# Query-key dots in float32r with split operands instead of float32 on half the array

## The chip, the cores and the metric

One core of a Trainium2 chip runs the whole program in one launch. The metric is the device time of that launch in microseconds, the median of several runs. A separate profiled execution gives the trace from which all rows below are taken.

## The reference, cut to what matters

Two layers run over a prompt of 1024 tokens and a sample of 64 tokens with 256 cached ones. In each layer the input projection feeds, among others, a ReLU indexer (4 heads of 64, one shared key), whose scores pick the top 256 keys, and a sparse attention (8 query heads of 64 over 2 key heads):

```python
rel = jax.nn.relu(jnp.einsum('bqhd,bsd->bqhs', qi_b, ki).astype(jnp.float32))
score = jnp.einsum('bqhs,bqh->bqs', rel, wi_b.astype(jnp.float32)) * IDX_SCALE
_, idx = lax.top_k(score, topk)
...
logits = jnp.einsum('bqngd,bqknd->bqngk', qg, kg).astype(jnp.float32) * (HD_A ** -0.5)
```

The retention heads, the gates, the norms and the output projection are not touched.

## The kernel before, in words

The work is a fixed sequence of 180 steps, 9 tiles of 128 tokens (t = 0 to 7 the prompt, t = 8 the sample) for each of 10 column groups in 2 layers: idx (324 columns), ret four times, gate, att twice, out twice. The order on every engine is written out by hand: a loop over i, in which TensorE projects the tile of step i+1 in four quarters (q = 0 to 3, two slices of the contraction each) and puts the work of older steps between the quarters. `project` makes each product in three float32r matmuls (high by high, low by high, high by low; the sample tile needs two).

A tile of idx or att goes this way. TensorE projects it; VectorE rotates it (`rope`, lines 1720 to 1737, through the scratch tile by_cos_sin); TensorE turns queries and keys in quarter 2 (line 996, into out_bank for idx, a turn bank for att); ScalarE copies them out (`take_turn`, lines 1363 and 1364) into queries and keys; in quarters 0 to 3 of the next i TensorE makes the dots (`dot_keys`, line 1044), always two heads at a time. One head's 64 features lie in partitions 0 to 63, the other's in 64 to 127, and a dot is one float32 matmul over its half. A tile has one or two parts of at most 512 keys; with one part there are dots in quarters 0 and 2, with two parts in all four. I call the dots of one part and two heads a pair. There are 22 pairs in the idx group of a layer and 26 in each att group, 148 in all: 72 of 512 keys, 32 of 384, 20 of 256, 4 of 320 and 20 of 128.

idx dots are taken by ScalarE (ReLU, line 1403) and weighed by VectorE (line 1756). att dots are masked and maximised by VectorE (line 1928). GpSimd makes the low halves of the weights (line 1554) and, in the idx groups, the low halves of the normed input h (line 1560, two for a tile), and the diagonals by which the raw input is normed while it is turned (lines 1593 to 1601). The weights of the next column group come one slice a step, t = 0 to 7, into w_hi and w_lo with 16 places (WS).

## Time and profile before

| what | us |
|---|---|
| median of 3 runs | 1431.36 (1430.39 to 1431.76) |
| the profiled execution | 1430.55 |
| its span, first to last instruction | 1428.7 |
| TensorE busy in it | 1380.3 (97%) |
| VectorE busy | 1010.9 (71%) |
| ScalarE busy | 783.7 (55%) |
| GpSimd busy | 405.2 (28%) |

Busy times of TensorE are modelled: matmuls overlap in the pipeline, so that the distance from one start to the next says more of the cost than the duration of one. A float32 matmul is two instructions in the trace. In a row of the timeline the first number is the start in us from the start of the span, the second the duration.

### The profile page before, as it was taken

The page shows a single profiled execution, that of the slowest core. Times are in us where ns is not written, and L with a number is a line of the kernel's source. Part 1 is how long each engine was busy: PE and PEld are TensorE (multiplying, and loading weights), DVE is VectorE, ACT ScalarE, POOL GpSimd, SP SyncE. Part 2 cuts the span into 40 slices and gives each one's busy share as a digit, 9 for nine tenths or more (in the row PEclk, how much of TensorE's full clock was granted, in tenths as well). Part 3 has the DMA queues.
Part 4 walks back from the last instruction along what each step waited for, and adds up shares of the span by engine and source line. Part 5 has one row for each costly group of instructions (what it writes and reads, how often), then busy time and mean ns, then how long its engine had stood idle before and what let it go on. Part 6 is the DMA issues. An engine that isn't in the chain of part 4 may idle for free.

```text
span 1428.7 us, 24483 instructions
## 1 busy us (share of the span) xinstructions
PE 1380.3 (97%) x7623; PEld 1054.7 (74%) x7623; DVE 1010.9 (71%) x2991; ACT 783.7 (55%) x1916; POOL 405.2 (28%) x382
## 2 busy tenths in 40 slices
PE   6999999999999999999988999999999999999997
PEld 2865777788887677668877587877888766766786
DVE  0787899999996555542398789999999754554225
ACT  2555666666326665664454566666632566666432
POOL 3741332444421011001387123443343100100110
PEclk9999999999999999999999999999999999999999
DMA  9743333211232112223252111211223211221325
GB/s 317 230 133 106 96 121 115 78 29 54 58 92 66 42 39 69 82 65 106 93 186 62 40 32 51 52 43 40 62 58 88 68 32 46 71 66 61 116 78 175
DMA packets 125191, 122.05 MB, mean 85 GB/s; under 512 B 33256, under 2 KB 94024, under 8 KB 125064
## 3 DMA queue, kind: packets, MB, share of 16 engines
q1 hardware_dynamic: 124608, 120.36, 28.1%
q8 instruction: 64, 1.05, 0.3%
q14 instruction: 63, 0.52, 0.1%
q10 hardware_dynamic: 456, 0.13, 0.0%
HBM read 93.55 MB, written 26.90 MB: 84 GB/s over the span
## 4 chain that ended last, share of the span: by engine, by line
PE 55%; DVE 33%; issue 5%; POOL 2%; DMA 2%; ACT 1%; DVEq 0%; ACTq 0%; SPq 0%; POOLq 0%
DVE U L1782 12%; PE proj L1017 10%; PE proj L1018 9%; PE turn L996 9%; PE proj L1020 9%; PE logit L1044 7%; PE out_bank L1071 5%; PE spare L1044 2%; DVE turned L1737 2%; DVE by_cos_sin L1722 2%; DVE by_cos_sin L1720 2%; DVE probsT_more L1855 2%; DVE probsT_more L1859 1%; POOL h_lo L1560 1%; DVE U L1876 1%
## 5 line engine op out<-in xcount | busy, mean ns | idle before, releaser
L1017 PE MATMUL proj<-w_hi,h_hi 128*128 128x512 f32 (+2 forms) x1440 | 574.4, 399 | 3.0 <-POOL h_lo L1560 2.2
L1018 PE MATMUL proj<-w_lo,h_hi 128*128 128x512 f32 (+2 forms) x1440 | 535.3, 372 | 0.0
L1020 PE MATMUL proj<-w_hi,h_lo 128*128 128x512 f32 (+2 forms) x1280 | 477.4, 373 | 0.0
L1554 POOL TENSOR_TENSOR w_lo<-w_raw,w_hi 128x512 fp32r<-128x512 f32 (+2 forms) x160 | 202.9, 1269 | 741.5 <-ACT w_hi L1260 741.3
L1017 PEld LDWEIGHTS proj<-w_hi,h_hi 128*128 128x128 f32 x1440 | 271.9, 189 | 53.3 <-issue 15.8
L1018 PEld LDWEIGHTS proj<-w_lo,h_hi 128*128 128x128 f32 x1440 | 272.1, 189 | 31.0
L1020 PEld LDWEIGHTS proj<-w_hi,h_lo 128*128 128x128 f32 x1280 | 240.2, 188 | 37.1
L1782 DVE TENSOR_SCALAR_CACHE_REDUCE U<-score,cand 128x384 bf16<-128x384 f32 x310 | 223.0, 752 | 2.4 <-DVE cand L1799 0.3
L1044 PE MATMUL logit<-keys,queries 64*128 64x512 f32 (+4 forms) x454 | 137.2, 542 | 2.3 <-ACT U L1403 1.6
L1383 ACT ACTIVATE probsT_more<-turn 128x512 f32<-128x512 f32 (+3 forms) x156 | 76.1, 491 | 96.0 <-PE turn L996 95.8
L996 PEld LDWEIGHTS turn<-ident,U 128*128 128x128 f32 x604 | 68.4, 140 | 52.7 <-issue 36.9
L996 PE MATMUL turn<-ident,U 128*128 128x128 f32 x604 | 97.4, 281 | 4.2 <-ACT probsT_more L1383 2.6
L1260 ACT ACTIVATE w_hi<-w_raw 128x512 fp32r<-128x512 f32 (+2 forms) x160 | 95.0, 595 | 11.4 <-DMA w_raw<-in_w_in_dram 11.4
L1416 ACT ACTIVATE U<-U,neg_max 128x384 f32<-128x384 f32 (+7 forms) x108 | 81.5, 755 | 23.5 <-DVE neg_max L1933 23.1
L1570 POOL TENSOR_TENSOR rstd<-means,minus_half 128x3 f32<-128x3 f32 (+2 forms) x42 | 32.2, 766 | 215.6 <-DVE means L1910 148.9
L1435 ACT ACTIVATE U<-score,cand 128x896 bf16<-128x896 f32 x62 | 64.6, 1043 | 34.6 <-DVE cand L1820 34.6
L1737 DVE TENSOR_TENSOR turned<-by_cos_sin 128x256 f32<-128x256 f32 (+1 forms) x126 | 71.6, 568 | 9.6
L1720 DVE TENSOR_TENSOR by_cos_sin<-rows,cos_b 128x256 f32<-128x256 f32 (+1 forms) x108 | 52.2, 484 | 35.9 <-ACT rows L1316 33.1
L1928 DVE CUSTOM_DVE_ANT_0 U<-logit,score 128x512 f32<-128x512 f32 (+3 forms) x71 | 41.2, 585 | 49.1 <-PE logit L1044 48.9
L1071 PE MATMUL out_bank<-probsT_more,U 128*64 128x256 f32 x468 | 75.2, 385 | 0.0
L1435 ACT ACTIVATE probsT_more<-score,cand 128x1024 bf16<-128x1024 f32 x62 | 70.4, 1136 | 0.0
L1044 PEld LDWEIGHTS logit<-keys,queries 64*128 64x128 f32 x454 | 44.4, 184 | 30.9 <-issue 27.8
(203 smaller groups left out, 2109.0 us busy)
## 6 DMA issues: line engine op xcount, KB each, us to landing
w_raw<-in_w_in_dram SPq DMA_DIRECT2D x80, 256.0 KB, 3.3
probsT_more<-in_w_ada_dram SPq DMA_DIRECT2D x64, 256.0 KB, 3.9
score<-mixed_dram SPq DMA_DIRECT2D x36, 256.0 KB, 3.0
score<-in_w_ada_dram SPq DMA_DIRECT2D x32, 256.0 KB, 5.1
w_raw<-in_w_out_dram SPq DMA_DIRECT2D x32, 256.0 KB, 3.4
U<-in_x_prompt_dram SPq DMA_DIRECT2D x12, 512.0 KB, 4.1
mixed_dram<-U SPq DMA_DIRECT2D x24, 192.0 KB, 2.1
gates_dram<-U SPq DMA_DIRECT2D x18, 256.0 KB, 2.1
```

The source lines that it names most:

```text
L996: ins = nc.tensor.transpose(ring.bank(key)[:, n * P:(n + 1) * P], piece, ident[:])
L1017: nc.tensor.matmul(out, h_hi[:, k, tile], hi, start=(k == 0), stop=False)
L1018: ins = nc.tensor.matmul(out, h_hi[:, k, tile], lo, start=False, stop=(t == SAMPLE and k == KT - 1))
L1020: ins = nc.tensor.matmul(out, h_lo[:, k, tile], hi, start=False, stop=(k == KT - 1))
L1044: ring.filled(nc.tensor.matmul(ring.bank(key)[:, 0:m], queries[rows_, HILO[g] % 2, h // 2, :], keys[rows_, k0 + a:k0 + a + m], start=True, ...
L1071: ins = nc.tensor.matmul(out_bank[HD * pair:HD * pair + HD, 0:256], v, probsT[part + pair][:, :, b * P:(b + 1) * P], start=(kb == 0), stop ...
L1260: nc.scalar.activation(w_hi[:, s % WS, 0:w], w_raw[:, n % RAWS, 0:w], ACT.Copy).then_inc(w_hi_ready, 1)
L1416: nc.scalar.activation(probs[n % 4][:, 0:w], probs[n % 4][:, 0:w], ACT.Exp, bias=neg_max[:, n % 4:n % 4 + 1], scale=ATT_SCALE, accum_out=r ...
L1435: nc.scalar.activation(tested[n % 2][:, 0:valid_keys(t)], scores(t)[:, 0:valid_keys(t)], ACT.Sign, bias=cand[:, col:col + 1].bitcast(F32) ...
L1554: nc.gpsimd.tensor_tensor(w_lo[:, s % WS, 0:w], w_raw[:, n % RAWS, 0:w], w_hi[:, s % WS, 0:w].bitcast(F32), ALU.subtract).then_inc(w_lo_re ...
L1737: signal(nc.vector.tensor_tensor(turned[:, ro % 2, 0:w], by_cos[:, 0:w], by_sin[:, 0:w], ALU.add), rope_done, ro + 1)
L1782: ins = nc.vector.tensor_scalar(found[:, n % 2, 0:valid_keys(t)], s, cand[:, j:j + 1].bitcast(F32) if b else 0.0, extra(t), ALU.is_ge, ALU ...
```

## The change

Keys are kept as a high and a low half in float32r (keys_hi, keys_lo), and a head's queries as one 128-row operand: its high half in the partitions it came in, its low half in the other 64. The turned keys already stand twice, in both halves of the partitions. A dot is then two float32r matmuls over all 128 rows, by keys_hi and by keys_lo, with the same queries. ScalarE first copies the turned tile raw into by_cos_sin (line 1419 of the changed kernel), then makes the high halves of the queries in two copies. GpSimd makes both halves of the keys (1630, 1632). The low halves of the queries are made by GpSimd in idx steps (1643, two subtractions) and by VectorE in att steps (1854, two). `rope` of the next tile uses the same scratch, so it waits for all of these. The two key halves need room, so WS goes from 16 to 14 and the last two slices of a column group (LATE = 2) are split only in the sample step of the group before, after its first quarter.

```diff
-WS = 2 * KT
+WS = 2 * KT - 2
+LATE = 2 * KT - WS
...
-        keys = sb("keys", [P, NKEYS])
-        queries = sb("queries", [P, 2, GROUP // 2, P])
+        keys_hi = sb("keys_hi", [P, NKEYS], F32R)
+        keys_lo = sb("keys_lo", [P, NKEYS], F32R)
+        queries = sb("queries", [P, 2, GROUP, P], F32R)
...
+        raw_turn = by_cos_sin[:, 0:384]
...
-                    rows_ = slice(HD * (h % 2), HD * (h % 2) + HD)
-                    ring.filled(nc.tensor.matmul(ring.bank(key)[:, 0:m], queries[rows_, HILO[g] % 2, h // 2, :],
-                                                   keys[rows_, k0 + a:k0 + a + m], start=True, stop=True), key)
+                    out, both_halves = ring.bank(key)[:, 0:m], queries[:, HILO[g] % 2, h, :]
+                    nc.tensor.matmul(out, both_halves, keys_hi[:, k0 + a:k0 + a + m], start=True, stop=False)
+                    ring.filled(nc.tensor.matmul(out, both_halves, keys_lo[:, k0 + a:k0 + a + m],
+                                                 start=False, stop=True), key)
...
-                    turns_of(g).wait_taken(pe, ("q", g))
+                    wait_queries_split(pe, HILO[g] + 1)
+                    pe.wait_ge(keys_split, HILO[g] + 1)
...
-                nc.scalar.activation(queries[:, HILO[g] % 2], src[:, 0:256].rearrange("p (h n) -> p h n", n=P), ACT.Copy)
-                ring.take(nc.scalar.activation(keys[:, blk * P:(blk + 1) * P], src[:, 256:384], ACT.Copy), ("q", g))
+                ring.take(nc.scalar.activation(raw_turn, src[:, 0:384], ACT.Copy), ("q", g))
+                ring.wait_taken(act, ("q", g))
+                for half in (0, 1):
+                    at = slice(HD * half, HD * half + HD)
+                    ins = nc.scalar.activation(queries[at, n % 2, half::2, :],
+                                               raw_turn[at, 0:256].rearrange("p (h n) -> p h n", n=P), ACT.Copy)
+                ins.then_inc(queries_high, 1)
...
-                if i + 1 < STEPS:
-                    if weight_slice(i + 1) is not None:
-                        split_weights(weight_slice(i + 1))
+                if early_slice(i + 1) is not None:
+                    split_weights(early_slice(i + 1))
                 for q in range(QUARTERS):
+                    if q == 1:
+                        for s in late_slices(i + 1):
+                            split_weights(s)
...
+                if kind(i) in ("idx", "att"):
+                    split_keys(i)
+                if kind(i) == "idx":
+                    lower_queries(i)
+                if has_cache_turn(i):
+                    split_cache(i)
...
+                if splits_before(g):
+                    wait_queries_split(dve, splits_before(g))
+                    dve.wait_ge(keys_split, splits_before(g))
...
+                if kind(i) == "att":
+                    lower_queries(i)
```

TensorE, the dots of quarter 0 of an idx tile with 512 keys, between two quarters of the projection of a later tile (logit is one of two banks). Before, then after:

```order
L1020 MATMUL proj<-w_hi,h_lo 128x324
L1044 MATMUL logit<-keys,queries 128x512 [waits logit_taken1,logit_taken0,idx_turn_taken]
L1044 MATMUL logit<-keys,queries 128x512
L1017 MATMUL proj<-w_hi,h_hi 128x324 [waits w_lo_ready]
L1018 MATMUL proj<-w_lo,h_hi 128x324
```

```order
L1066 MATMUL proj<-w_hi,h_lo 128x324
L1092 MATMUL logit<-keys_hi,queries 128x512 [waits logit_taken0,logit_taken1,keys_split,index_split]
L1093 MATMUL logit<-keys_lo,queries 128x512
L1092 MATMUL logit<-keys_hi,queries 128x512
L1093 MATMUL logit<-keys_lo,queries 128x512
L1063 MATMUL proj<-w_hi,h_hi 128x324 [waits w_lo_ready]
```

Two matmuls became four, and the wait on ScalarE's copy became one on GpSimd's keys and low queries.

GpSimd, one step of the idx group of the first layer (the three operations on input_mean, input_root and score make one diagonal). Before, then after:

```order
L1601 TENSOR_SCALAR score<-ident,input_root 128x128 [waits input_rooted,turn_full0]
L1554 TENSOR_TENSOR w_lo<-w_raw,w_hi 128x512 [waits w_hi_ready]
L1560 TENSOR_TENSOR h_lo<-U,h_hi 128x4x128 [waits h_hi_ready] x2
L1593 TENSOR_SCALAR input_mean<-squares 128x1 [waits x_squared]
L1596 TENSOR_TENSOR input_root<-input_mean,minus_half 128x1 [waits input_summed]
```

```order
L1614 TENSOR_TENSOR w_lo<-w_raw,w_hi 128x512 [waits w_hi_ready]
L1620 TENSOR_TENSOR h_lo<-U,h_hi 128x4x128 [waits h_hi_ready] x2
L1630 CAST keys_hi<-by_cos_sin 128x128 [waits idx_turn_taken]
L1632 TENSOR_TENSOR keys_lo<-by_cos_sin,keys_hi 128x128 [waits keys_high]
L1643 TENSOR_TENSOR queries<-by_cos_sin,queries 64x2x128 [waits keys_split,queries_high]
L1643 TENSOR_TENSOR queries<-by_cos_sin,queries 64x2x128 [waits index_split]
L1690 TENSOR_SCALAR input_mean<-squares 128x1 [waits x_squared,index_split]
```

Four operations stand behind the two low halves of h and ahead of everything of the next step.

VectorE, the first tile of the first att group. The operations on probsT_more and ties are the last selection mask. Before, then after:

```order
L1720 TENSOR_TENSOR by_cos_sin<-rows,cos_b 128x320 [waits rope_done,proj_taken]
L1722 TENSOR_TENSOR by_cos_sin<-rows,sin_b 128x320
L1735 TENSOR_TENSOR turned<-by_cos_sin 128x64 [waits dve_done,key_stored1,turn_full0]
L1737 TENSOR_TENSOR turned<-by_cos_sin 128x320
L1851 TENSOR_SCALAR probsT_more,ties<-score,cand 128x320 [waits rope_done]
```

```order
L1845 TENSOR_TENSOR turned<-by_cos_sin 128x320
L1854 TENSOR_TENSOR queries<-by_cos_sin,queries 64x2x128 [waits queries_high]
L1854 TENSOR_TENSOR queries<-by_cos_sin,queries 64x2x128
L1972 TENSOR_SCALAR probsT_more,ties<-score,cand 128x320 [waits queries_split]
L1973 TENSOR_SCALAR probsT_more<-score,cand 128x320
```

The two subtractions wait for the turn of this very tile, and the last mask now stands behind them.

## Rows read from the trace of the kernel before

**Rows 1.** Windows by stage: stretch, length, each engine's busy us, TensorE's granted clock.

```profile
38.74:127.90 89.16, 85.20 (x529) 61.21 (x529) 71.64 (x155) 47.46 (x124) 43.84 (x47) 1.00 0.53 160
419.44:651.96 232.52, 230.00 (x1454) 165.68 (x1452) 130.54 (x427) 146.12 (x381) 23.09 (x19) 1.00 0.21 59
743.04:829.10 86.06, 78.18 (x435) 55.70 (x434) 68.73 (x140) 44.27 (x111) 37.09 (x34) 1.00 0.23 58
```

**Rows 2.** Timeline of TensorE in an att step; start, us, line, tiles, shapes, count.

```profile
501.86 0.34 PE L1020 MATMUL proj<-w_hi,h_lo 128*128 128x384 f32 x1
502.04 0.60 PE L996 MATMUL turn<-ident,U 128*128 128x128 f32 x4
502.57 0.69 PE L1044 MATMUL logit<-keys,queries 64*128 64x512 f32 x1
502.57 0.69 PE L1044 MATMUL spare<-keys,queries 64*128 64x512 f32 x1
503.10 0.59 PE L1044 MATMUL logit<-keys,queries 64*128 64x512 f32 x1
...
503.63 0.55 PE L996 MATMUL turn<-ident,U 128*128 128x128 f32 x3
...
505.59 1.13 PE L1044 MATMUL logit<-keys,queries 64*128 64x512 f32 x4
...
511.48 0.34 PE L1020 MATMUL proj<-w_hi,h_lo 128*128 128x384 f32 x1
511.75 0.69 PE L1044 MATMUL logit<-keys,queries 64*128 64x512 f32 x1
```

**Rows 3.** Timeline of TensorE, two float32r matmuls of 512 columns.

```profile
643.24 0.39 PE L1020 MATMUL proj<-w_hi,h_lo 128*128 128x512 f32 x1
643.47 0.40 PE L1017 MATMUL proj<-w_hi,h_hi 128*128 128x512 f32 x1
```

**Rows 4.** Groups by shape, GpSimd and VectorE: count, busy us, mean ns, idle before.

```profile
L1554 POOL TENSOR_TENSOR w_lo<-w_raw,w_hi 128x512 fp32r<-128x512 f32 x112 | 147.7, 1319 | 579.8 <-ACT w_hi L1260 579.7
L1554 POOL TENSOR_TENSOR w_lo<-w_raw,w_hi 128x324 fp32r<-128x324 f32 x16 | 14.3, 902 | 15.9 <-ACT w_hi L1260 15.9
L1601 POOL TENSOR_SCALAR score<-ident,input_root 128x128 f32<-128x128 f32 x9 | 5.6, 622 | 1.4 <-POOL input_root L1596 1.2
```

```profile
L1953 DVE TENSOR_TENSOR score<-score 128x256 f32<-128x256 f32 x36 | 15.3, 426 | 3.7
```

**Rows 5.** Timeline of an idx step of the first layer (tile 4).

```profile
83.77 0.39 ACT L1363 ACTIVATE queries<-out_bank 128x256 f32<-128x256 f32 x1
...
84.18 1.17 ACT L1268 ACTIVATE h_hi<-U 128x512 fp32r<-128x512 f32 x2
...
84.92 2.52 POOL L1560 TENSOR_TENSOR h_lo<-U,h_hi 128x512 fp32r<-128x512 f32 x2 [3.68 <-ACT h_hi L1268]
...
87.54 0.70 PE L1044 MATMUL logit<-keys,queries 64*128 64x512 f32 x2
```

**Rows 6.** Chain of work, idx group of the second layer: start, us, what.

```profile
754.20 2.90 POOL h_lo L1560 x2
...
760.14 2.47 POOL h_lo L1560 x2
...
768.32 1.60 DVE turned L1737
```

**Rows 7.** Timeline of an idx step of the second layer (tile 3).

```profile
779.23 0.39 ACT L1363 ACTIVATE queries<-out_bank 128x256 f32<-128x256 f32 x1
...
780.64 0.70 PE L1044 MATMUL logit<-keys,queries 64*128 64x512 f32 x2
```

**Rows 8.** Timeline, first tile of the first att group.

```profile
428.12 0.38 ACT L1363 ACTIVATE queries<-turn 128x256 f32<-128x256 f32 x1 [3.34 <-PE turn L996]
...
430.10 0.49 PE L1044 MATMUL logit<-keys,queries 64*128 64x128 f32 x4
...
430.33 1.30 DVE L1720 TENSOR_TENSOR by_cos_sin<-rows,cos_b 128x320 f32<-128x320 f32 x1
```

More of the change, by code:

```diff
@@ L304, in weight_slice, with early_slice, late_slices @@
     return (C + 1) * KT + t if t < KT and C + 1 < DEPTH * NCH else None
+def early_slice(g):
+    return weight_slice(g) if 0 <= g < STEPS and g % NT < KT - LATE else None
+def late_slices(g):
+    return [weight_slice(g - n) for n in range(LATE, 0, -1)] \
+        if 0 <= g < STEPS and g % NT == SAMPLE and g // NT + 1 < DEPTH * NCH else []
 def raw_items():
@@ L627, in build @@
         turn_taken = [sem(f"turn_taken{n}") for n in range(RB)]
+        queries_high = sem("queries_high")
+        queries_split = sem("queries_split")
+        index_split = sem("index_split")
+        keys_high = sem("keys_high")
+        keys_split = sem("keys_split")
+        cache_high = sem("cache_high")
+        cache_split = sem("cache_split")
+        first_quarter = sem("first_quarter")
         idx_turned = sem("idx_turned")
@@ L678, in ring_of, with cache_ordinal, splits_before, wait_queries_split @@
             return att_logits if kind(g) == "att" else logits
+        def cache_ordinal(g):
+            return sum(1 for k in range(g + 1) if has_cache_turn(k))
+        def splits_before(g):
+            return sum(1 for k in HILO if k < g)
+        def wait_queries_split(eng, n):
+            last = [g for g in HILO_STEPS[:n]]
+            index = 2 * sum(1 for g in last if kind(g) == "idx")
+            if index:
+                eng.wait_ge(index_split, index)
+            if len(last) * 2 > index:
+                eng.wait_ge(queries_split, len(last) - index // 2)
         def hidden_half(l, t, u):
@@ L761, in wait_keys_free, with wait_cache_free @@
                         ring_of(j).wait_full(eng, ("l", j, 3, len(key_parts(held)) - 1))
+        def wait_cache_free(eng, g):
+            if HILO[g] >= NT:
+                j = HILO_STEPS[HILO[g] - NT + 1]
+                n = valid_keys(SAMPLE) if kind(j) == "idx" else blocks_of(SAMPLE)[1] * P
+                ring_of(j).wait_full(eng, ("l", j, 3, len(key_parts(n)) - 1))
         def raw_value(n):
@@ L877, in _ @@
                     l, c, t = lct(i + 1)
-                    before = [k for k in range(i + 1) if has_cache_turn(k)]
-                    if before:
-                        turns.wait_full(sp, ("cache", before[-1]))
+                    if cache_ordinal(i):
+                        sp.wait_ge(cache_split, cache_ordinal(i))
                     src = cache_kidx_a[l, 0] if kind(i + 1) == "idx" else cache_k_a[l, 0, :, c - ATT0, :]
@@ L1020, in project @@
                         ins = nc.tensor.matmul(out, h_lo[:, k, tile], hi, start=False, stop=(k == KT - 1))
+                if quarter == 0 and t == SAMPLE:
+                    ins.then_inc(first_quarter, 1)
                 if quarter == QUARTERS - 1:
@@ L1257, in split_weights @@
                 act.wait_ge(raw_landed[n % RAWS], raw_value(n))
-                if C >= 2:
+                if s % KT >= KT - LATE and C:
+                    act.wait_ge(first_quarter, C)
+                elif C >= 2:
                     act.wait_ge(proj_done, (C - 1) * NT)
@@ L1281, in take_projection @@
                     act.wait_ge(rope_done, sum(1 for k in ROPE if k < g))
+                    if splits_before(g):
+                        wait_queries_split(act, splits_before(g))
+                        act.wait_ge(keys_split, splits_before(g))
                     nc.scalar.activation(sample_low[:, 0:w], src[DEC:P, 0:w], ACT.Copy).then_inc(low_copied, 1)
@@ L1643, in _ @@
                     lower_hidden(0, 1)
-                if i + 1 < STEPS and weight_slice(i + 1) is not None:
-                    lower_weights(weight_slice(i + 1))
+                if early_slice(i + 1) is not None:
+                    lower_weights(early_slice(i + 1))
+                for s in late_slices(i + 1):
+                    lower_weights(s)
                 for l, t in hidden_turns(i - 1):
@@ L1738, in rope, with lower_queries @@
                        rope_done, ro + 1)
+            def lower_queries(g):
+                n = HILO[g]
+                dve.wait_ge(queries_high, n + 1)
+                for half in (0, 1):
+                    have, other = (slice(HD * h, HD * h + HD) for h in (half, 1 - half))
+                    ins = nc.vector.tensor_tensor(queries[other, n % 2, half::2, :],
+                                                  raw_turn[have, 0:256].rearrange("p (h n) -> p h n", n=P),
+                                                  queries[have, n % 2, half::2, :].bitcast(F32), ALU.subtract)
+                    if half == 0:
+                        do(ins)
+                signal(ins, queries_split, ATT[g] + 1)
             def weigh_relus(g, q):
```

49 lines of the change are left out of this document (40 added, 9 removed).

## The prediction

> **What bounds the kernel now.** I read the windows by stage first, then TensorE's timeline. The windows say that TensorE is the bound almost everywhere: in the first layer's attention (two att groups and their tail) it is busy 230.0 of 232.5 us, while VectorE, ScalarE and GpSimd have 130.5, 146.1 and 23.1 [rows 1]. The second layer's attention is the same. In the idx group of layer 0 TensorE has 85.2 of 89.2 us; in that of layer 1 only 78.2 of 86.1, and the chain there runs over GpSimd's low halves of h, from 754 on, and then over VectorE's rotation at 768 [rows 6]. So a microsecond less on TensorE is a microsecond less of time in the att groups, and not in the opening of the idx groups.
>
> The timeline gives what a pair of dots costs. Both heads start at the same 502.57, their second instructions at 503.10, and the next turn starts at 503.63: a pair of 512 keys holds TensorE 1.06 us [rows 2]. The four records of such a pair take 1.13 from first start to last end [rows 2], those of a pair of 128 keys 0.49 [rows 8], so 384 keys cost 0.64, and a pair of 384, 256 and 128 costs 0.85, 0.63 and 0.42. Getting in costs extra: a projection matmul of 384 columns passes in 0.18 (501.86 to 502.04), but the last before dots takes 0.27 (511.48 to 511.75); and of four turns that take 0.11 each the last takes about 0.20 (502.04 to 502.57 is 0.53) [rows 2]. That is 0.09 a pair. On the way out three turns end a full 0.55 after their start, against 0.60 for four [rows 2], some 0.06 more than in a stream. I read this as the price of going between the full array and its two halves.
>
> **What TensorE gains.** Four float32r matmuls replace the pair. One of 512 columns passes in 0.23 [rows 3], one of 384 in 0.18, so by the 0.055 for 128 columns one of 256 in 0.12; one of 128 columns I put at 0.11, the pace of the turns, since its weights have to come in too. Pairs of 512, 384, 256 and 128 then cost 0.92, 0.70, 0.48 and 0.44: gains of 0.14, 0.15, 0.15 and -0.02. The operands have all 128 rows like the projection's, so I take it that the 0.09 in and the 0.06 out go too: 0.29, 0.30, 0.30 and 0.13 a pair. The 104 att pairs (48 of 512, 24 of 384, 16 of 256, 16 of 128) give 13.9 + 7.2 + 4.8 + 2.1 = **28 us**, the 44 idx pairs (24, 8, 4, 4, and 4 of 320) 7.0 + 2.4 + 1.2 + 0.5 + 1.2 = **12 us**. The trace shows no float32r matmul under 324 columns; were the short ones four times as dear as by width, 20 pairs would cost 0.4 more, 8 us. If the way in and out stays as dear as now, the att gain is 13 us.
>
> The Trainium skill speaks against this edit. "TensorE: Matmul & The Clock Gate", Part 3, says that small matmuls on different row groups run concurrently, at some 4 ns between starts, and "FP8 and Floating Point Precision", TensorE Precision Notes, counts four passes for float32. By these two the pair costs 4 x 512 / 2.4 GHz = 0.85 us (an estimate) and four float32r matmuls as much, so nothing is gained. The trace agrees on the concurrency (502.57 twice) and not on the sum, 1.06.
>
> **The link that is added, att.** Counted from ScalarE's copy (line 1363), the dots were ready 0.65 later. Now the raw copy of 384 takes some 0.50 (256 take 0.38 in rows 8, 128 more add 0.11), a wait on it 0.1, two copies of 64 partitions 0.7: 1.3. Then VectorE's two subtractions, 0.43 each by a 256-wide one [rows 4], give 2.2; beside them GpSimd makes the keys in 1.2. TensorE comes to the dots 1.98 after the copy in tile 0 of the first att group [rows 8]; later tiles have more work between, so I cost them at nothing, the cover being a quarter of projection and the values. In tile 0, VectorE also waits for the turn of this tile, with the last mask queued behind it: its rotation is over before the turn, and the high halves come 1.3 after 428.12, so it stands idle some 2 us and works 0.9 more, and the next rotation, at 430.33 before, comes that much later [rows 8]. I put 3 us a layer on this, **6 us**, between 1 and 10.
>
> **The same link, idx.** Here GpSimd does four operations in a row. 512 columns take it 1.32, 324 take 0.90 [rows 4], so 256 take about 0.8 and 128 about 0.55; the cast, between nothing known and the 0.62 of a 128-wide scaling [rows 4], 0.5. With the two of 256 that is 2.65, and with three hand-overs of 0.1 some 3.1 us (bounds 2.4 and 4.0, as VectorE gets in between).
>
> Layer 0: the four stand behind two low halves of h, which wait for ScalarE, which makes them after the queries. In tile 4, the copy starts at 83.77 and GpSimd's halves at 84.92 for 2.52 [rows 5]. ScalarE's part is 0.65 longer now, so those end at 88.1 and the four at 91.2; TensorE stood at the dots at 87.54 [rows 5], now 0.3 earlier. It waits 4.0 us. Five tiles (2 to 6) have this shape: 19 us. Tiles 7 and 8 have no halves of h ahead, 1 us. Tiles 0 and 1 have no dots, but the next rotation waits for the four: 3.5 us each. Together 27, less 6 gained: **+21 us**.
>
> Layer 1: the chain is on GpSimd already [rows 6], and the four operations of tiles 0, 1 and partly 2 are inserted in it: 3.1 + 3.1 + 1.8 = 8. From tile 3 on the dots came 1.41 after the copy [rows 7], and they need 0.5 + 0.1 + 3.1 = 3.7 now, less 0.3 that TensorE comes sooner: 2.5 us of wait, shrinking to about 1 at tile 8, 11 us for six tiles. Together 19, less 6: **+13 us**. VectorE's rotation, held by GpSimd in this stretch (1.60 for 320 columns where 256 take 0.43 elsewhere [rows 4, 6]), is likely to be held more often; I leave that in the bounds.
>
> The Trainium skill has the mechanism: "SBUF — State Buffer" calls the port pair of VectorE and GpSimd an exclusive lock, which a VectorE instruction with two SBUF inputs takes too. By that each of GpSimd's four could also wait for one of VectorE's; the 4.0 above covers it.
>
> **Late slices.** ScalarE gets two weight copies and GpSimd two subtractions (2 x 1.32, rows 4) in one step instead of two. They are needed a full step later, so the weights are not late; ScalarE's queue is. 19 times 0.15 us: **+3 us**, between 0 and 8.
>
> **Sum.** -28 + 6 + 21 + 13 + 3 = +15 on the profiled 1430.55, which is 1445.6. The median was 0.8 above the profiled run, so 1446.
>
> **Rivals.** (a) The link is hidden better than I think: GpSimd's four take 2.4 and VectorE's stretches shrink as much as TensorE's. That takes 17 x 0.7 = 12 us off, and with half of the opening waits gone another 8: 1425. For it: TensorE's gain is certain, GpSimd is idle 72% of the time. Against: the distances of 1.41 and 3.77 are read directly. (b) Slower still: each of the four waits for one VectorE operation, 4.0 instead of 3.1, in 17 tiles 15 us more: 1460. It decides from the point where VectorE weighs ReLUs without a pause in the idx steps (71.6 of 89.2 us busy, rows 1). (c) No price for going in and out of the half array is saved, or the skill's rule holds and only that is: the att gain is 13 to 15, the idx gain 6, so 1462. (d) The granted clock is 1.00 in all three stretches [rows 1]; waits of 4 us in a row of steps may let it fall to the lower level, and projections at half pace for 3 us in six steps cost some 12: 1457. "TensorE: Matmul & The Clock Gate", Part 1, says that idleness brings the clock down to 1.2 GHz; no run here shows it. (e) The dots never wait, since the saved work arrives elsewhere: 1430.55 - 40 + 9 = 1400.
>
> **Chances.** Forecast 0.50, (a) 0.20, (b) 0.09, (c) 0.09, (d) 0.07, (e) 0.05. The range holds the forecast's own bounds and most of (a) to (d): 1420 to 1466. What a measurement of this kernel can tell from no change is about 0.2%, 2.9 us. Faster: (e) and most of (a), 0.20; the same 0.09; slower 0.71.
>
> **What would show it.** In the new trace the four dot matmuls of 512 keys should pass in 0.92 with no 0.27 ahead of them; the att stretches should last about 220 us instead of 232.5. In layer 0's idx group TensorE's first dots should wait 4 us a tile on GpSimd's queries, and the stretch should last 110 us instead of 89; in layer 1 99 instead of 86. If att steps wait on VectorE's subtractions, or the idx stretch does not grow, I am wrong.

## The result, and where the time went

| | us | ratio to before, 95% interval | profiled execution | span |
|---|---|---|---|---|
| before | 1430.93 (1430.39 to 1431.76) | | 1430.55 | 1428.7 |
| changed | 1466.05 (1463.46 to 1471.63) | 1.0249 (1.0224 to 1.0275) | 1463.46 | 1461.6 |

The change makes the kernel 35.1 us slower, where the prediction had 15 (1446, within 1420 to 1466). The direction was right and the forecast less than half of what came. The profiled execution, the fastest of four, is 32.9 slower than the one before, and the account below is made with it.

The windows of the changed kernel over the same three stretches as in [rows 1] (stretch, length, busy us and counts of TensorE, its weight loads, VectorE, ScalarE and GpSimd, then TensorE's granted clock, DMA share and GB/s):

```profile
38.43:153.58 115.15, 91.15 (x530) 75.45 (x530) 66.34 (x155) 55.94 (x134) 64.69 (x84) 0.93 0.40 123
446.64:675.02 228.38, 219.11 (x1454) 184.55 (x1452) 147.60 (x463) 160.66 (x399) 40.55 (x61) 1.00 0.21 61
765.21:864.91 99.70, 80.90 (x435) 71.38 (x433) 72.66 (x140) 51.77 (x120) 64.23 (x74) 0.91 0.21 53
```

Against [rows 1] the idx stretch of layer 0 grew from 89.16 to 115.15, that of layer 1 from 86.06 to 99.70, and the attention of a layer shrank from 232.52 to 228.38. With the other layer's attention (232.71 to 228.42 between the same steps) that is +26.0 + 13.6 - 4.1 - 4.3 = +31.2; the remaining 1.7 lie in the ret and out steps between. The clock is the second thing to read: it was 1.00 in all three stretches of before and is 0.93 and 0.91 in the two idx stretches now.

TensorE's waits in the changed kernel (who waited for whom, total us, times, longest):

```profile
PE logit L1092 <- POOL queries L1643: 23.0, 12, 2.6
...
PE out_bank L1042 <- DVE turned L1845: 8.6, 4, 2.8
PE turn L1042 <- DVE turned L1845: 8.2, 11, 1.7
PE turn L1042 <- ACT probsT_more L1441: 6.7, 16, 1.0
PE proj L1063 <- POOL h_lo L1620: 4.5, 7, 1.1
```

The first row is the link that the change added: idx dots that wait for GpSimd's low halves of the queries. The waits for rotated tiles (the two rows with `turned`) are 16.8 us in all, where they were 9.1 before: VectorE's rotation stands idle for the same subtractions, 46.2 us in 14 places, because it needs the scratch that they read. One tile (t = 3 of layer 0), in the timeline of the changed kernel (start, us, then engine, line, operation):

```profile
84.01 2.51 POOL L1620 TENSOR_TENSOR h_lo<-U,h_hi 128x512 fp32r<-128x512 f32 x2 [3.80 <-ACT h_hi L1320]
...
86.47 0.29 POOL L1630 CAST keys_hi<-by_cos_sin 128x128 fp32r<-128x128 f32 x1
86.84 0.45 POOL L1632 TENSOR_TENSOR keys_lo<-by_cos_sin,keys_hi 128x128 fp32r<-128x128 f32 x1
87.44 1.51 POOL L1643 TENSOR_TENSOR queries<-by_cos_sin,queries 64x256 fp32r<-64x256 f32 x2
89.00 0.79 PE L1092 MATMUL logit<-keys_hi,queries 128*128 128x512 f32 x1 [2.52 <-POOL queries L1643]
89.04 0.49 DVE L1828 TENSOR_TENSOR by_cos_sin<-proj,cos_b 128x320 f32<-128x320 f32 x1 [5.17 <-POOL queries L1643]
...
89.60 0.63 PE L1093 MATMUL logit<-keys_lo,queries 128*128 128x512 f32 x1
90.02 0.63 PE L1092 MATMUL logit<-keys_hi,queries 128*128 128x512 f32 x1
...
90.45 0.63 PE L1093 MATMUL logit<-keys_lo,queries 128*128 128x512 f32 x1
...
90.88 0.47 PE L1063 MATMUL proj<-w_hi,h_hi 128*128 128x324 f32 x1
91.14 0.47 PE L1064 MATMUL proj<-w_lo,h_hi 128*128 128x324 f32 x1
```

GpSimd's four operations stand behind the two low halves of h, as predicted, and take 86.47 to 88.95, 2.5 us (the prediction had 3.1). TensorE waits 2.52 for them, and VectorE, whose next rotation needs the scratch, has been idle for 5.17. After the wait the dots of 512 keys start 0.43 apart and the projections of 324 columns 0.27, where the same matmuls stand 0.23 and 0.15 apart elsewhere: TensorE is at the lower of its two levels (1.2 GHz).

The dots themselves do what was forecast. TensorE in an att step of the changed kernel, coming from the projection:

```profile
537.57 0.33 PE L1066 MATMUL proj<-w_hi,h_lo 128*128 128x384 f32 x1
537.74 0.39 PE L1092 MATMUL logit<-keys_hi,queries 128*128 128x512 f32 x1
537.97 0.40 PE L1093 MATMUL logit<-keys_lo,queries 128*128 128x512 f32 x1
538.20 0.40 PE L1092 MATMUL spare<-keys_hi,queries 128*128 128x512 f32 x1
538.44 0.39 PE L1093 MATMUL spare<-keys_lo,queries 128*128 128x512 f32 x1
538.76 0.43 PE L1120 MATMUL out_bank<-U 128*64 128x256 f32 x1
```

The last projection passes in 0.17 instead of the 0.27 of [rows 2], and the dots stand 0.23 apart. Only the last, ahead of the value matmuls (which use 64 columns of the array), takes 0.32; before, a pair went over to them without a surcharge. So 512 keys cost 0.92, and 1.01 ahead of values, instead of 1.06. Of the 148 pairs 16 stand ahead of values, all of them in the att groups.

### The profile page after: what moved, and what is told of

Same layout as the page of the kernel before. It is cut to its first block and busy times, and to the rows that moved or that the text cites. A ratio compares the mean times of both kernels' runs of the same rounds, so it can differ in the third digit from the quotient of the medians.

```text
span 1461.6 us, 25157 instructions
## 1 busy us (share of the span) xinstructions
PE 1367.4 (94%) x7623; PEld 1122.7 (77%) x7623; DVE 1043.0 (71%) x3063; ACT 828.2 (57%) x1970; POOL 480.3 (33%) x538
## 5 line engine op out<-in xcount | busy, mean ns | idle before, releaser
L1614 POOL TENSOR_TENSOR w_lo<-w_raw,w_hi 128x512 fp32r<-128x512 f32 (+2 forms) x160 | 199.9, 1255 | 525.9 <-ACT w_hi L1312 525.8
L1092 PE MATMUL logit<-keys_hi,queries 128*128 128x512 f32 (+4 forms) x227 | 86.0, 383 | 27.3 <-POOL queries L1643 23.0
L1630 POOL CAST keys_hi<-by_cos_sin 128x128 fp32r<-128x128 f32 x54 | 17.7, 327 | 246.7 <-ACT by_cos_sin L1419 246.7
L1312 ACT ACTIVATE w_hi<-w_raw 128x512 fp32r<-128x512 f32 (+2 forms) x160 | 92.6, 592 | 10.1 <-DMA w_raw<-in_w_in_dram 9.2
L1093 PE MATMUL logit<-keys_lo,queries 128*128 128x512 f32 (+4 forms) x227 | 80.9, 361 | 0.0
L1092 PEld LDWEIGHTS logit<-keys_hi,queries 128*128 128x128 f32 x227 | 44.9, 198 | 40.7 <-POOL queries L1643 26.7
L1845 DVE TENSOR_TENSOR turned<-by_cos_sin 128x256 f32<-128x256 f32 (+1 forms) x126 | 67.7, 537 | 9.9 <-DVE by_cos_sin L1830 0.5
L1461 ACT ACTIVATE U<-logit 128x512 f32<-128x512 f32 (+4 forms) x66 | 33.2, 532 | 71.1 <-PE logit L1093 71.1
```

Of the source, the lines that this page charges most:

```text
L1092: nc.tensor.matmul(out, both_halves, keys_hi[:, k0 + a:k0 + a + m], start=True, stop=False)
L1093: ring.filled(nc.tensor.matmul(out, both_halves, keys_lo[:, k0 + a:k0 + a + m], start=False, stop=True), key)
L1312: nc.scalar.activation(w_hi[:, s % WS, 0:w], w_raw[:, n % RAWS, 0:w], ACT.Copy).then_inc(w_hi_ready, 1)
L1614: nc.gpsimd.tensor_tensor(w_lo[:, s % WS, 0:w], w_raw[:, n % RAWS, 0:w], w_hi[:, s % WS, 0:w].bitcast(F32), ALU.subtract).then_inc(w_lo_re ...
```

## The experiments

**The dots alone (e1).** The kernel before, with TensorE's new matmuls and nothing else of the change. It leaves out the low halves and mixes the two heads of a pair, so that its logits, and what follows from them, are other numbers:

```diff
-        keys = sb("keys", [P, NKEYS])
-        queries = sb("queries", [P, 2, GROUP // 2, P])
+        keys = sb("keys", [P, NKEYS], F32R)
+        queries = sb("queries", [P, 2, GROUP // 2, P], F32R)
...
-                    ring.filled(nc.tensor.matmul(ring.bank(key)[:, 0:m], queries[rows_, HILO[g] % 2, h // 2, :],
-                                                   keys[rows_, k0 + a:k0 + a + m], start=True, stop=True), key)
+                    for n in (0, 1):
+                        ins = nc.tensor.matmul(ring.bank(key)[:, 0:m], queries[:, HILO[g] % 2, h // 2, :],
+                                               keys[:, k0 + a:k0 + a + m], start=(n == 0), stop=(n == 1))
+                    ring.filled(ins, key)
```

> The kernel before, in which a dot is two float32r matmuls over all 128 rows (the two heads of a pair mixed, no low halves, so the logits are others): TensorE has exactly the matmuls of the changed kernel, and the copies, the waits and the weight slices are those of before. Theory A (the gain on TensorE is real, 0.28 us a pair or 13 us in the att groups of a layer and 6 in an idx group, and new waits eat it): 1430.9 - 26 - 12 = 1393, at most 1400, and no step of the att groups loses. Theory B (the gain itself is small, 0.1 a pair): 1430.9 - 15 = 1416. Theory C (TensorE only comes too early to the turns of the probabilities, which ScalarE and VectorE make at a pace of their own): the waits of the heavy att tiles stand here too, some 7 us a layer of the gain is lost: 1407.

Measured: 1397.89 us, ratio 0.9767 (0.9752 to 0.9781), 33.3 below. The windows of this kernel over the three stretches:

```profile
38.95:124.38 85.43, 81.47 (x529) 69.17 (x530) 72.07 (x155) 47.89 (x125) 44.98 (x47) 1.00 0.55 167
415.09:635.72 220.63, 217.54 (x1453) 184.89 (x1451) 131.88 (x427) 146.34 (x381) 22.98 (x19) 1.00 0.22 62
726.66:807.89 81.23, 73.94 (x434) 65.61 (x433) 69.36 (x139) 44.72 (x111) 37.13 (x34) 0.98 0.25 61
```

Against [rows 1]: -3.7, -11.9 and -4.8. Theory A holds for att. The gain is there, 11.9 of the 14 that the prediction had for a layer. Only 4 of it is left in the changed kernel, so what else was changed takes it away again. Theory B, a small gain, is out. In idx the gain is 8.5 over these stretches. The stretch of layer 0 in [rows 1] ends one step before that group's last dots, where another 0.8 is gained (8.90 to 8.11), so that the idx gain is 9.3 and not 12.

**The chain alone (e2).** The changed kernel, with the old pair of float32 matmuls on the high halves; the low halves are made and waited for, but left out of the dots:

```diff
-                    nc.tensor.matmul(out, both_halves, keys_hi[:, k0 + a:k0 + a + m], start=True, stop=False)
-                    ring.filled(nc.tensor.matmul(out, both_halves, keys_lo[:, k0 + a:k0 + a + m],
-                                                 start=False, stop=True), key)
+                    ring.filled(nc.tensor.matmul(out, queries[rows_, HILO[g] % 2, h, :].bitcast(F32),
+                                                   keys_hi[rows_, k0 + a:k0 + a + m].bitcast(F32),
+                                                   start=True, stop=True), key)
```

> The changed kernel with its dots made as before, one float32 matmul a head on half the array, from the high halves alone (the low halves are made and waited for, but no dot reads them): the whole chain and the late slices without the gain. Theory A (the chain costs): 12 more than the changed kernel in the idx groups less what TensorE no longer waits, and in att the waits of tile 0 and of the tiles 5 to 8 stay: 1466 + 12 + 26 - 8 = 1496 at most, 1480 at least. Theory C (early arrival makes the waits of the heavy att tiles): TensorE comes late again and the heavy tiles are as long as before, only tile 0 costs 3 us a layer: 1472 to 1478.

Measured: 1506.64 us, 1.0532 (1.0513 to 1.0551), 75.4 above before and more than either theory gave.

```profile
39.44:163.55 124.11, 99.46 (x529) 67.10 (x529) 65.99 (x155) 55.12 (x133) 64.48 (x84) 0.88 0.38 115
457.38:697.69 240.31, 231.00 (x1453) 165.53 (x1451) 147.16 (x463) 160.45 (x399) 40.41 (x61) 1.00 0.20 58
787.52:893.21 105.69, 87.23 (x434) 63.78 (x433) 72.92 (x140) 51.49 (x120) 63.49 (x74) 0.90 0.19 50
```

These windows are over the same stretches. The chain costs 35.0 and 19.6 in idx and 7.8 in this layer's attention (8.9 in the other's). Theory C, that TensorE only arrives too early, is out twice: e1 arrives early and keeps its gain, e2 arrives late and still loses. The two parts alone add up to +42 (-33.3 and +75.4), and together they give +35, so they are not quite independent.

**Late slices alone (e3).** The kernel before with 14 places for weights, which is the part of the change from `early_slice` to `late_slices` and nothing more:

```diff
-WS = 2 * KT
+WS = 2 * KT - 2
+LATE = 2 * KT - WS
```

> The kernel before with the last two weight slices of each column group split late (14 places instead of 16), and nothing else. Prediction's term: +3 us over 19 groups, 1434. Theory A2 (the two copies stand in ScalarE's queue ahead of the probabilities in the sample step of the two att groups, where TensorE waits 0.9 and 1.1 in the changed kernel): +3.5 in ret and out groups and 2 to 4 in each layer's att groups: 1438 to 1441.

Measured: 1435.25 us, 1.0030 (1.0018 to 1.0042), +4.0: the forecast's +3 was near. The places were in part others. The sample steps of the two att groups of each layer are 0.6 and 0.8 longer, and the second step of the first att group is 0.8 shorter. The profiled execution of e3, 5.6 above that of before, has another 2.0 in layer 1's idx stretch (88.01, where the granted clock was 0.98) and 0.9 ahead of the first step. The changed kernel's timeline in the sample step of the first att group:

```profile
517.09 0.92 ACT L1312 ACTIVATE w_hi<-w_raw 128x384 fp32r<-128x384 f32 x2
...
517.92 0.86 ACT L1441 ACTIVATE probsT_more<-turn 128x512 f32<-128x512 f32 x2
...
518.65 0.41 PE L1042 MATMUL turn<-ident,U 128*128 128x128 f32 x2 [0.72 <-ACT probsT_more L1441]
```

Two weight copies in a row hold up the copies of the turned probabilities, and TensorE waits 0.72 for a bank. In e3, without the rest of the change, it waits 0.43 here.

**float32r in att only (e4).** The changed kernel, with the idx groups' copies and float32 dots as before, in tiles that lie over the same memory:

```diff
+                if kind(g) == "idx":
+                    wait_keys_free(act, g)
+                    nc.scalar.activation(idx_queries[:, n % 2],
+                                         src[:, 0:256].rearrange("p (h n) -> p h n", n=P), ACT.Copy)
+                    ring.take(nc.scalar.activation(idx_keys[:, blk * P:(blk + 1) * P], src[:, 256:384],
+                                                   ACT.Copy), ("q", g))
+                    return
...
-                if kind(i) in ("idx", "att"):
-                    split_keys(i)
-                if kind(i) == "idx":
-                    lower_queries(i)
+                if kind(i) == "att":
+                    split_keys(i)
```

> The changed kernel in the att groups, and in the idx groups the copies and float32 dots of before; GpSimd and the low halves of queries have no part in idx steps. If the two links are independent, the idx groups are as long as before (77.7 and 67.4 us instead of 103.2 and 80.6) and the time is 1466.0 - 38.7 = 1427, or 1424.8 by the profiled execution: 3 to 6 us below the kernel before. If the idx groups have pushed work into the ret groups behind them, it is 2 to 3 us more or less.

Measured: 1426.94 us, 0.9972 (0.9961 to 0.9982): 4.3 below the kernel before and 39.1 below the changed one. The idx stretches are back at 89.95 and 88.08, 0.8 and 2.0 above before (0.5 and 2.0 in e3). So the loss is the idx groups', and the att part with the late slices is a small gain.

**VectorE lowers the idx queries (e5), GpSimd splits ahead of h (e6), both (e13).**

```diff
-                if kind(i) == "att":
+                if kind(i) in ("idx", "att"):
                     lower_queries(i)
```

> The changed kernel, in which VectorE makes the low halves of the queries in the idx groups too (at the end of its step's work, as in att), so that GpSimd has only the two operations on the keys. GpSimd's pair took 1.51 us in tile 4. Theory A (GpSimd's queue is what makes the dots late in idx): the dots come up to 1.5 us sooner a tile and the clock falls less: 1466 - 10 to 18 = 1450 to 1456. Theory B (VectorE's own queue, with the ReLUs ahead of the subtractions, is as late as GpSimd's): 1466 or up to 10 more.

```diff
+                if kind(i) in ("idx", "att"):
+                    split_keys(i)
+                if kind(i) == "idx":
+                    lower_queries(i)
                 for l, t in hidden_turns(i - 1):
                     if l == 0 and i >= 0:
                         lower_hidden(l, t)
```

> The changed kernel, in which GpSimd makes the halves of the keys and queries before the two low halves of h in layer 0's idx steps. The dots waited 2.7 us on GpSimd and GpSimd had 2.5 us of h ahead. Theory A (the order in GpSimd's queue sets the wait): the dots' wait is gone in tiles 2 to 6, the low halves of h come 2.5 later instead and the projection waits for them at the next step's start: half of layer 0's 25 us comes back, 1450 to 1455. Theory B (GpSimd's whole work per step sets the pace): the wait moves to the projection and the time stays at 1463 to 1468.

> The changed kernel with both idx edits that gained 7 to 8 us each: VectorE makes the low queries, and GpSimd makes the key halves ahead of the low halves of h. If they take away the same wait, 1455 to 1458; if they add, 1450. In either case the idx groups stay over 10 us a layer longer than with the plain float32 dots, so float32r dots do not pay there: above 1431.

Measured: e5 1458.23 us, 1.0186 (1.0171 to 1.0201); e6 1458.88, 1.0189 (1.0168 to 1.0210); e13 1453.90, 1.0158 (1.0142 to 1.0173). Each gives back 7 to 8, both 12, and each ended between its two theories. In e5 the nine steps of layer 0's idx group are 13.9 shorter, but the two behind them 5.1 longer, and layer 1's idx stretch is only 0.7 shorter. The dots now wait for VectorE's subtractions, 18.6 us in 12 places where they waited 23.0 for GpSimd's. In e6 the wait changed its name, as its theory B had it, but only in part. TensorE's waits in e6:

```profile
PE proj L1063 <- POOL h_lo L1620: 14.0, 7, 3.6
PE logit L1092 <- POOL queries L1643: 10.1, 7, 2.3
```

The queries cost 10.1 instead of 23.0, the low halves of h 14.0 instead of 4.5.

**The two subtractions left out (e14).** The changed kernel, in which the idx queries have no low halves, so that this small part of the dots is missing:

```diff
-                if kind(i) == "idx":
-                    lower_queries(i)
```

> The changed kernel, in which the idx groups leave the low halves of the queries out (the idx dots are then a little less exact): GpSimd has only the two operations on the keys there, and nobody makes the other two. Theory A (GpSimd's queue is the chain): each tile gains the 1.5 us of the pair and some clock, 17 tiles: 25 us or more of the 38.7 come back, 1436 to 1441. Theory B (ScalarE's raw copy, its two half copies and the shared scratch are the larger part): at most 12 come back, 1454.

Measured: 1440.17 us, 1.0058 (1.0041 to 1.0075), 25.9 below the changed kernel. Theory A holds. Two of the four operations that GpSimd got in each idx step, 1.5 us a tile, are worth 15.0 us in layer 0's idx stretch (115.15 to 100.13) and 11.9 in layer 1's (99.70 to 87.78), the clock included. The windows of e14 over these two:

```profile
39.79:139.92 100.13, 87.05 (x529) 71.90 (x530) 66.47 (x155) 55.82 (x134) 53.24 (x67) 0.97 0.46 142
...
753.28:841.06 87.78, 75.25 (x435) 65.64 (x433) 72.43 (x139) 51.92 (x120) 50.49 (x56) 0.98 0.23 59
```

The clock is at 0.97 and 0.98 instead of 0.93 and 0.91.

**Idle matmuls in the wait (e9, e15).** Ten, or six, matmuls whose result is written over, ahead of the wait of the first idx dots:

```diff
+                if q == 0 and kind(g) == "idx" and t in SEARCHED:
+                    first = ("l", g, *dots_at(g + 1, q)[0])
+                    logits.wait_free(pe, first)
+                    for n in range(10):
+                        nc.tensor.matmul(logits.bank(first)[:, 0:512], h_hi[:, n % 4, t * P:(t + 1) * P],
+                                         h_hi[:, 0:4, t * P:(t + 1) * P], start=True, stop=True)
```

> The changed kernel with ten float32r matmuls of 512 columns (0.23 us each, 2.3 us) ahead of TensorE's wait for the queries in each idx tile that has dots; their result is written over by the dots. They do nothing but keep TensorE at work while it would wait 2.7 us. Clock theory (a good part of the loss in idx is TensorE at the lower clock: 0.79 to 0.89 granted in ten of the steps, about 17 us of work lost by 1 - clock times length): the granted clock stays at 1.00, and the time falls to 1450 to 1456 although work is added. Rival (the chain over GpSimd sets the pace and the clock costs nothing on top): 1464 to 1470.

> e9_filler with six idle matmuls (1.4 us) instead of ten (2.3 us) ahead of each wait of the idx dots. Clock theory: with 1.3 us left of the wait the clock mostly stays up and the added work is hidden in the wait everywhere, so that the time is 4 to 8 us below the changed kernel: 1458 to 1462. If it falls all the same, 1464 to 1468.

Measured: e9 1465.56 us, 1.0234 (1.0217 to 1.0251), the same as the changed kernel; e15 1462.77, 1.0221 (1.0206 to 1.0237), 3.3 below it, with intervals that overlap. By the times e9 ended where the rival put it, and e15 between its two theories. The medians settle nothing about the clock, the steps do. Four steps of layer 0's idx group, first of the changed kernel, then of e15, then the first two of e9:

```profile
85.33:99.53 14.20, 11.22 (x63) 9.11 (x64) 7.36 (x19) 6.22 (x15) 7.70 (x11) 0.88 0.31 96
99.53:115.53 16.00, 13.04 (x68) 10.71 (x68) 8.19 (x19) 6.08 (x15) 4.64 (x7) 0.79 0.21 68
115.53:129.70 14.17, 10.41 (x56) 8.27 (x56) 9.35 (x22) 5.48 (x14) 4.19 (x7) 0.88 0.31 92
129.70:141.63 11.93, 9.29 (x46) 7.30 (x46) 7.67 (x15) 5.15 (x11) 6.26 (x9) 0.86 0.24 65
```

```profile
87.28:100.03 12.75, 11.34 (x69) 8.90 (x69) 8.34 (x19) 6.14 (x15) 7.72 (x11) 1.00 0.35 108
100.03:113.44 13.41, 11.81 (x74) 9.37 (x74) 8.12 (x19) 5.93 (x15) 4.66 (x7) 1.00 0.25 81
113.44:126.27 12.83, 10.42 (x62) 7.99 (x62) 9.35 (x22) 5.40 (x14) 4.22 (x7) 1.00 0.35 104
126.27:137.09 10.82, 9.35 (x51) 7.07 (x52) 8.05 (x15) 4.93 (x11) 6.76 (x9) 1.00 0.22 57
```

```profile
87.43:100.21 12.78, 12.27 (x74) 9.67 (x74) 8.35 (x19) 6.12 (x15) 7.73 (x11) 1.00 0.38 111
100.21:113.65 13.44, 12.77 (x78) 10.13 (x78) 8.11 (x19) 5.92 (x15) 4.67 (x7) 1.00 0.25 82
```

With work added, the four steps take 49.81 instead of 56.30 us, at a clock of 1.00. So 6.5 us of layer 0's loss is the lower clock. That six or ten idle matmuls give the same length says that at full clock these steps are set by the chain and not by TensorE. In layer 1 nothing is won: e15 has 99.67 us at a clock of 0.97 against 99.70 at 0.91, and e9 104.09. There most of the time at the lower clock lies in the first steps, which got no idle matmuls, so what it costs there stays open. In the dots of the last tile the six idle matmuls aren't hidden: they add 1.4 us in layer 0 and 1.6 in layer 1.

**The opening of att (e7).** e4, with VectorE's mask ahead of its subtractions in the first att tile:

```diff
-                if kind(i) == "att":
+                if kind(i) == "att" and kind(j) == "att":
                     lower_queries(i)
...
+                if kind(i) == "att" and kind(j) != "att":
+                    lower_queries(i)
                 if roots_first(i):
```

> e4_att_only, in which VectorE makes the low queries of the first att tile after the last mask instead of before it. e4 has a step that is 2.7 and 3.1 us longer than before in this place. If the row maxima are late because the mask stands behind VectorE's wait for this tile's turn, those come back, 5 to 6 us in both layers together: 1421 to 1422. If the dots are then late themselves (they need the subtractions), about 1426 as e4.

Measured: 1425.37 us, 0.9958 (0.9943 to 0.9973), 1.6 below e4; by the profiled steps 1.0 in layer 0 and 2.2 in layer 1, where the clock had fallen in e4 (0.90 over these two steps) and not in e7 (1.00). Against the changed kernel, whose clock was 1.00 here in both layers, it is 1.1 a layer. That is less than half of what the first theory gave, and the intervals of e4 and e7 overlap. The rest stays since the dots now wait for the subtractions themselves. TensorE in e7 at this place:

```profile
435.02 0.33 PE L1101 MATMUL logit<-keys_hi,queries 128*128 128x128 f32 x1 [2.01 <-DVE queries L1879]
...
435.74 0.34 PE L1066 MATMUL proj<-w_lo,h_hi 128*128 128x384 f32 x1
435.92 0.33 PE L1068 MATMUL proj<-w_hi,h_lo 128*128 128x384 f32 x1
```

**Slices apart (e8), a scratch of its own (e10), both (e12).** Each on top of e7:

```diff
-                    if q == 1:
-                        for s in late_slices(i + 1):
-                            split_weights(s)
+                    for s in late_slices(i + 1)[q // 2:q // 2 + 1]:
+                        if q % 2:
+                            split_weights(s)
```

> e7_att_mask_first with the two late weight slices apart: ScalarE copies the first in the second quarter and the second in the last quarter of the sample step, and GpSimd subtracts the second after the keys. In e7 TensorE waits 0.88 and 1.09 us in the sample steps of the two att groups behind two weight copies in a row; in the dots-only kernel 0.06 in both. Theory: 0.5 to 0.8 us comes back in each of the four sample steps and a little in ret: 1425.4 - 3 = 1422.5. Rival (the second copy is in the way wherever it stands): 1425 to 1426.

```diff
-        raw_turn = by_cos_sin[:, 0:384]
+        def raw_turn(g):
+            return score[:, 3584:3968] if lct(g)[1] == ATT0 else by_cos_sin[:, 0:384]
```

> e7_att_mask_first, in which the raw copy of the first att group of a layer has columns of its own (free there) instead of the rotation's scratch, so that neither the next rotation nor ScalarE's copy in the sample step waits for the low queries. In e7 ScalarE waits 1.03 us for the subtractions there and TensorE then 0.65 for the turned probabilities. Theory (the shared scratch makes these waits): the steps behind the sample tile of the first att group get back 0.6 to 0.7 us a layer, and the second att group, which still shares, changes by nothing: 1424. Rival (VectorE's and ScalarE's added work itself is in the way): no step changes by more than 0.2.

> e8_late_spread and e10_own_scratch together. If the two are independent, both gains add: 1421 to 1422, 0.65% below the kernel before.

Measured: e8 1425.95 us, 0.9964 (0.9951 to 0.9977); e10 1425.77, 0.9961 (0.9947 to 0.9976); e12 1424.87, 0.9951 (0.9935 to 0.9968). None can be told from e7's 1425.37. In e8 the sample steps of the att groups get back 0.4 and 0.5, and the steps behind the sample tiles of idx and of the first att group lose 0.6 to 0.7: this is the rival's outcome, that a weight copy is in ScalarE's way wherever it stands. In e10 the step behind the first att group's sample tile is 0.7 and 0.6 shorter, as expected of the shared scratch. The expectation's 0.65 for TensorE's wait there is 0.49 in e7's trace. The opening of att is 1.6 longer in both layers, though, with the same wait. TensorE in e10, the place shown above for e7:

```profile
434.50 0.33 PE L1109 MATMUL logit<-keys_hi,queries 128*128 128x128 f32 x1 [2.01 <-DVE queries L1887]
...
435.54 0.52 PE L1074 MATMUL proj<-w_lo,h_hi 128*128 128x384 f32 x1
435.86 0.52 PE L1076 MATMUL proj<-w_hi,h_lo 128*128 128x384 f32 x1
```

The wait is 2.01 in both. In e7 the projections behind it start 0.18 apart, in e10 0.32: there the clock fell. It fell at this place in both layers of e10 and of e12 (0.90 over the two steps) and in neither of e7 and e8 (1.00). Each is one profiled execution, so whether the scratch of its own brings it about was not shown.

## Why the prediction was wrong

Its terms against what the runs measured (e1 for the gains, the changed kernel less e1 for the links, both over the idx and att stretches and the step behind layer 0's idx stretch, the links without e3's share):

| term | forecast | measured |
|---|---|---|
| TensorE in att | -28 | -24 (232.5 to 220.6, twice) |
| TensorE in idx | -12 | -9.3 (3.7 + 0.8 and 4.8) |
| link in att | +6 | +14 (228.38 - 220.63, less 0.6, and the same in layer 1) |
| link in idx | 27 + 19 = +46 | +46 (29.7 + 18.5, less 2.5) |
| late slices | +3 | +4.0 (medians) |
| what remains | 0 | +2.2 |
| sum | +15 | +33 |

**The step that failed most** is "later tiles have more work between, so I cost them at nothing". The link in att costs 7 us a layer and not 3. The opening, which the forecast had at 3, takes 3.2 of it. The other 4 lie in the tiles that were costed at nothing: 0.8 in the two steps from the first group's sample tile on, and 2.9 in the last two steps of the second group and the one behind. One place is this, in the changed kernel's timeline behind the sample tile of the first att group:

```profile
525.21 1.24 DVE L1854 TENSOR_TENSOR queries<-by_cos_sin,queries 64x256 fp32r<-64x256 f32 x2
...
526.64 0.49 ACT L1337 ACTIVATE by_cos_sin<-proj 64x384 f32<-64x384 f32 x1 [1.03 <-DVE queries L1854]
...
528.94 0.41 PE L1042 MATMUL turn<-ident,U 128*128 128x128 f32 x2 [0.50 <-ACT U L1441]
```

ScalarE copies the sample tile's lower half (`sample_low`) through the scratch that the raw copy uses, so it waits 1.03 us for VectorE's subtractions, and TensorE 0.50 for the turned probabilities behind that. e10 takes this away in one of the two groups, and 0.6 to 0.7 us with it. The next place is the last but one step of the second att group, 0.9 longer than in e1. The changed kernel there:

```profile
613.23 0.87 DVE L1854 TENSOR_TENSOR queries<-by_cos_sin,queries 64x256 fp32r<-64x256 f32 x2
614.13 1.29 DVE L2102 TENSOR_TENSOR h_lo<-turn,h_hi 128x512 fp32r<-128x512 f32 x2
614.97 0.30 PE L1042 MATMUL turn<-ident,U 128*128 128x128 f32 x1 [0.78 <-DVE h_lo L2102]
```

VectorE makes the low halves of the mixed rows right behind its two subtractions (0.87), and TensorE waits 0.78 for them. Before, and in e1, it has no such wait; in e2, which has the subtractions, it is 1.00. The step behind, 1.7 longer than e1 and e3 account for, has several waits: 0.48 of the same kind, 0.93 for the turned probabilities behind the two late weight copies (before 0.24, in e3 0.64), and 0.29 and 0.66 for ScalarE's raw copy and its copy of the cached keys (before 0.35 for the one copy). What each of these is worth alone no run shows. I had asked only whether the dots are ready in time, and not what else stands behind the subtractions in VectorE's queue and behind the longer copies in ScalarE's.

**TensorE's gain was taken too high**, by 4 in att and 3 in idx. The two prices of [rows 2] go as forecast, except ahead of the value matmuls, where a new one appears (0.32 instead of 0.23); with 16 such pairs that is 1.4 us, so the rest of the 4 stays open. In e1 the idx dots wait 3.1 us for ScalarE's ReLUs where they waited 1.8 before, which is half of the 3. The mechanism, 0.92 for 512 keys and no 0.27, was right. The estimate that the prediction made from "TensorE: Matmul & The Clock Gate", Part 3, of the Trainium skill and four passes for float32, by which nothing would be gained, is not borne out: e1 gains 33 us.

**The idx link** came out at its size by luck, from errors that cancel. GpSimd's four operations took 2.5 in nine of the 18 tiles and 2.7 to 3.2 in the others, where I had 3.1, and TensorE waited 1.9 a time (23.0 in 12) where I had 4.0 and 2.5, 31 in all. Against that stands the clock, 6.5 us in layer 0 and an unknown part in layer 1, which the forecast had at nothing. That was rival (d), which I gave 0.07 and priced apart from the forecast, at 12. It belonged into the sum, since the waits of 4.0 us forecast for five tiles in a row are the waits that (d) asks for. The Trainium skill's rule in "TensorE: Matmul & The Clock Gate", Part 1, was cited there as one that no run shows; the trace of the changed kernel now agrees with it, with a granted clock of 0.79 to 0.89 in ten of the idx steps.

**Profiled time and median.** The prediction added 0.8. The four runs of the changed kernel go from 1463.46 at a mean clock of 0.987 to 1471.63 at 0.978, and the median is 2.6 above the profiled one. The executions differ more than before (8.2 between the ends here, 1.4 there), and the longest one had the lowest clock.

**Right:** the sign, that the loss sits in idx and the gain in att, the order in GpSimd's queue behind the halves of h (e6 and e14 bear it out), the size of the late slices. Layer 1's idx stretch was put at 99 and is 99.7; layer 0's at 110 and is 115.2; the att stretches at 220 and are 228.4, which e1 alone reaches. Rival (b), VectorE in GpSimd's way, is not what makes the loss: GpSimd's pair of subtractions took 1.51 to 1.55 in 14 of 18 tiles and at most 1.87, and twice the least that one takes is 1.43.

**Slips in the prediction's sums.** Rival (c), with 13 to 15 less from att and 6 less from idx, comes to 1465 to 1467 and not to 1462. That is the measured time, but e1 shows that its mechanism is wrong. Half pace for 3 us in six steps loses 9 in rival (d) and not 12. 2.65 and three hand-overs of 0.1 are 2.95 and not 3.1, and five waits of 4.0 are 20 and not 19.

**Better than both kernels:** float32r in att only, with the mask first: 1425.37 (e7), or 1424.87 with e12's edits, 0.4 and 0.5% below before. e4 shows that what counts is to leave idx out. A scratch of its own for the raw copy of the idx groups, for which VectorE's rotation waits there, was not tried.

## What to carry to other kernels

A matmul that is cheaper but needs prepared operands is worth its gain only where the preparing engine has slack at that place: here, apart from the late slices, it won 10 us net in the att groups, where GpSimd had 23 and VectorE 131 of 232 us of work, and lost 36 net in the idx groups, where the new step stood in a queue that was already waited for. When a step is added to a queue, ask of each engine what stands behind it and who shares its scratch, above all in the odd tile (the sample here), and not only whether its own result comes in time. When a forecast has TensorE waiting in step after step (here 1.9 us on average in twelve idx tiles), price the lower clock into the forecast itself.

## What the runs showed of the hardware that was not expected

- After the same wait of 2.01 us at the same place the clock stayed up in one kernel and fell in the other (projections of 384 columns 0.18 and 0.32 apart). So it is not the length of this one wait alone that decides, and whether the clock falls is worth 1.6 us at this place. It fell in both layers of e10 and e12 and in neither of e7 and e8; what decides it was not shown.
- Matmuls that do nothing can pay: 1.4 us of them in each wait made four steps 6.5 us shorter in all, though the whole kernel did not become faster beyond the noise.
- Between float32 turns and float32r dots of 512 keys the last turn passes in 0.03 and the first dot takes 0.31 (31 places in the changed kernel), together as much as in a stream; between float32r dots and value matmuls on 64 columns the last dot takes 0.32 instead of 0.23.
- GpSimd's cast of 128 columns takes 0.29, its subtraction of 128 columns 0.46 and of 64 partitions by 256 0.72 (medians).
